# A two-block transformer kernel: the first input loaded a second time in turned layout, scaled, rounded and split by chunk

## The chip, the cores and the metric

One core of one Trainium2 chip. The metric is the device time of one launch in microseconds (us), as the median of several runs. The program names its engines as the profile does: PE (TensorE, the matrix engine), ACT (ScalarE), DVE (VectorE), POOL (GpSimd) and SP (SyncE, which here only issues DMAs).

## The reference

The program computes two transformer blocks, one after the other, on 256 tokens of width 1024, in float32. Only the start of the first block matters here:

```python
def rms_norm(x, g):
    y = x * lax.rsqrt(jnp.mean(x * x, axis=-1, keepdims=True) + EPS)
    return y * g

xn = rms_norm(x, ln_mix_g)           # x: 256 x 1024
proj = xn @ w_in                     # w_in: 1024 x 2560, five blocks of 512 columns
u, v, q, k, vv = five blocks of proj # columns 0.., 512.., 1024.., 1536.., 2048..
a_out = gelu(u) * spatial(rms_norm(gelu(v)))
b_out = banded attention(q, k, vv)
x = x + concat(a_out, b_out) @ w_out
x = x + peer_ffn(rms_norm(x))        # each token gathers 128 rows of a table of experts
```

A second block follows (`second_block`: a pooling branch, a stick-breaking attention, a cross attention, gates and a feed-forward layer). It is untouched by the change.

## The kernel before

**Tiles.** The 256 tokens are two tiles `t` of 128 (`tok(t)`), the width of 1024 is eight chunks `c` of 128. The product of tokens with `w_in` has the chunk's 128 channels on the partitions, so `x` is wanted turned: `aT_hi` and `aT_lo` are 128 partitions x 8 chunks x 256 tokens. The division by the root mean square of a token is put off: it is a factor of a row of the product and is applied after it (`row_scale`, line 857 on). Only the gain `ln_mix_g`, one number per channel (`mix_col`, on the partitions), is multiplied in ahead of the product.

**Three products for one.** To keep float32 accuracy, each operand is split into a rounded part (type fp32r, "hi", ACT) and the rest ("lo", DVE), and `product` (lines 1970 to 1972) issues three matmuls: hi x hi, hi x lo, lo x hi. So every weight block goes through DMA into `wraw` (four slots of 1 MB), a cast on ACT into `w_hi` (line 806), a subtraction on DVE into `w_lo` (line 1288), then PE. A block is half of the 1024 rows of one 512-column part: `in1a` holds chunks 0 to 3, `in1b` chunks 4 to 7 of the first part. Order of the blocks: in1a, in1b, in2a, in2b, in3a, in3b, in4a, in4b, in0a, in0b. Each is 24 matmuls of 512 columns (4 chunks x 2 token tiles x 3). The split has three slots (`S_SLOTS`), and a slot of `wraw` is loaded again when the DVE subtraction of the block in it is done (`load_block`). The blocks in `PIECED` (line 66) are loaded, cast and subtracted in four quarters of 256 KB, one chunk each (lines 618, 813, 1296), and PE waits for each quarter; the others go whole.

**The order of the work** is written out by hand, one list of instructions for each engine, with semaphores between them. At the start:

- SP issues one small load (`const`: the identity, and the columns of the two gains), x tile 0, two quarters of in1a, x tile 1, two more, the four of in1b, then in2a, in2b whole, the rest of the constants, and in3a.
- PE multiplies the identity with itself six times (`keep_warm`, line 1948; 12 records), turns x tile 0 through the identity (`turn_x`, eight transposes at line 1941, into two banks of PSUM), begins in1a, and after its first chunk turns x tile 1 (`between_at=1`).
- DVE multiplies each turned half tile of 128 x 512 by the gain, out of PSUM into `xg` (`gained_T`, line 1326), ACT rounds it into `aT_hi` (`round_x`, line 848), DVE subtracts into `aT_lo` (`rest_x`, line 1333). These steps stand among the quarters of in1a.
- When the splits of in1b and in2a are through, ACT squares and sums x tile 0 and tile 1 from `x_sb` (line 764), takes the roots (line 771), loads the table of the gelu (line 790), casts in2b, takes the gelu of the first product (line 871), squares it, loads the table of the root, and casts in3a and in3b.

After this come attention, the output product, the router, and then `for n in range(ROWS)` 256 gathers of 128 table rows of 8 KB on POOL's queue, each with one dot product on DVE, small steps on ACT and matmuls on PE (line 2284), and after them the second block.

## Time and profile before

| | us |
|---|---|
| median of three runs | 1153.95 |
| lowest, highest | 1153.13, 1154.22 |
| span of the profiled execution, first to last instruction | 1151.8 |

The page gives the profiled execution by its span alone; no device time of its own stands beside it. Shares of the span: PE busy 91%, DVE 67%, ACT 49%, POOL 25%. The chain of waits that ended last runs through PE for 57% of the span and through the DMAs of the gathers for 28%.

How to read it: a timeline row is start, duration, engine, line, operation, operands, count; in brackets the idle time of the engine just before, and what ended it. Durations include what the engine overlaps with the next instruction, so the distance between two starts is often smaller than a duration. PEclk is the clock granted to PE as a share of full speed (1.00 is 2.4 GHz, 0.50 is 1.2 GHz).

### The profile page before, as it was taken

The page shows a single profiled execution, that of the slowest core. Times are in us where ns is not written, and L with a number is a line of the kernel's source. Part 1 is how long each engine was busy: PE and PEld are TensorE (multiplying, and loading weights), DVE is VectorE, ACT ScalarE, POOL GpSimd, SP SyncE. Part 2 cuts the span into 40 slices and gives each one's busy share as a digit, 9 for nine tenths or more (in the row PEclk, how much of TensorE's full clock was granted, in tenths as well). Part 3 has the DMA queues.
Part 4 walks back from the last instruction along what each step waited for, and adds up shares of the span by engine and source line. Part 5 has one row for each costly group of instructions (what it writes and reads, how often), then busy time and mean ns, then how long its engine had stood idle before and what let it go on. Part 6 is the DMA issues. An engine that isn't in the chain of part 4 may idle for free.

```text
span 1151.8 us, 12055 instructions
## 1 busy us (share of the span) xinstructions
PE 1048.5 (91%) x4100; PEld 669.5 (58%) x4100; DVE 770.0 (67%) x1502; ACT 567.0 (49%) x1235; POOL 290.9 (25%) x261
## 2 busy tenths in 40 slices
PE   8999998998899779799887877889999999999998
PEld 7888554454354234344332322349878778888886
DVE  5788777667666657676676665564675496777743
ACT  7664544544543444543444345354765555444432
POOL 0001545544544334454443444400000000000000
PEclk9999999999999999999999999999999999999999
DMA  9848999999999999999999999977433454555540
GB/s 346 346 161 306 420 422 422 421 421 422 421 420 422 420 422 421 411 421 423 422 419 422 423 420 422 422 307 270 181 147 135 157 189 159 183 188 193 195 156 36
DMA packets 55532, 371.87 MB, mean 323 GB/s; under 512 B 6192, under 2 KB 7344, under 8 KB 12080
## 3 DMA queue, kind: packets, MB, share of 16 engines
q0 software_dynamic: 36864, 268.45, 56.1%
q1 hardware_dynamic: 18608, 102.65, 24.1%
q8 instruction: 33, 0.54, 0.2%
q14 instruction: 27, 0.22, 0.1%
HBM read 370.03 MB, written 1.05 MB: 322 GB/s over the span
## 4 chain that ended last, share of the span: by engine, by line
PE 57%; DMA 28%; DVE 6%; ACT 5%; issue 2%; POOL 1%; DVEq 0%; POOLq 0%; ACTq 0%
DMA uv<-in_peer_uv,eidx 28%; PE bank L2284 15%; PE bank L1970 8%; PE bank L1972 8%; PE bank L1971 8%; PE bank L2460 6%; PE bank L2042 4%; PE bank L2459 3%; DVE uv L1579 2%; DVE w_lo L1288 1%; PE bank L1941 1%; ACT diag L1026 1%; POOL uv L730 1%; ACT chosen L1023 1%; PE bank L2160 1%
## 5 line engine op out<-in xcount | busy, mean ns | idle before, releaser
L2284 PE MATMUL bank<-uv,diag 128*128 128x512 f32 x1024 | 486.9, 610 | 89.6 <-ACT diag L1026 89.3
L1579 DVE SCALAR_TENSOR_TENSOR uv<-uv,xn 128x1024 f32<-128x1024 f32 x256 | 313.8, 1226 | 211.7 <-DMA uv<-in_peer_uv,eidx 211.6
L730 POOL DMA_INDIRECT uv<-in_peer_uv,eidx x256 | 290.6, 1135 | 456.3 <-PE bank L2284 329.2
L2284 PEld LDWEIGHTS bank<-uv,diag 128*128 128x128 f32 x1024 | 183.9, 192 | 355.5 <-issue 353.4
L1288 DVE TENSOR_TENSOR w_lo<-wraw,w_hi 128x2048 fp32r<-128x2048 f32 x69 | 157.7, 2290 | 92.2 <-ACT w_hi L806 92.1
L1018 ACT ACTIVATE chosen<-chosen 128x1 f32<-128x1 f32 x256 | 51.8, 202 | 331.7 <-DVE uv L1579 331.3
L806 ACT CAST w_hi<-wraw 128x2048 fp32r<-128x2048 f32 x69 | 131.6, 1908 | 123.6 <-PE bank L2460 62.0
L2460 PE MATMUL bank<-nT_both,w_hi 128*128 128x512 f32 x320 | 109.6, 396 | 0.0
L1026 ACT ACTIVATE diag<-const,chosen 128x128 f32<-128x128 f32 x256 | 102.8, 401 | 8.3
L1023 ACT ACTIVATE chosen<-chosen 128x1 f32<-128x1 f32 x256 | 75.3, 294 | 9.3
L2459 PE MATMUL bank<-nT_both,w_lo 128*128 128x256 f32 x280 | 78.1, 279 | 0.0
L2460 PEld LDWEIGHTS bank<-nT_both,w_hi 128*128 128x128 f32 x320 | 57.3, 188 | 10.8
L1970 PE MATMUL bank<-w_hi,nT_both 128*128 128x512 f32 x144 | 58.0, 403 | 0.9 <-ACT gates L1166 0.6
L1972 PE MATMUL bank<-w_hi,nT_both 128*128 128x512 f32 x144 | 56.2, 390 | 0.0
L1971 PE MATMUL bank<-w_lo,nT_both 128*128 128x512 f32 x144 | 56.2, 390 | 0.0
L2459 PEld LDWEIGHTS bank<-nT_both,w_lo 128*128 128x128 f32 x280 | 52.8, 188 | 1.8
L1970 PE MATMUL bank<-w_hi,aT_hi 128*128 128x512 f32 x104 | 42.1, 404 | 1.8 <-DVE aT_lo L1333 1.8
L1972 PE MATMUL bank<-w_hi,aT_lo 128*128 128x512 f32 x104 | 40.8, 393 | 0.0
L1971 PE MATMUL bank<-w_lo,aT_hi 128*128 128x512 f32 x104 | 40.8, 392 | 0.0
L2042 PEld LDWEIGHTS bank<-bT,wraw 128*128 128x128 f32 x192 | 30.4, 191 | 11.5 <-issue 9.6
L2042 PE MATMUL bank<-bT,wraw 128*128 128x128 f32 (+1 forms) x192 | 34.8, 327 | 0.0
L1970 PE MATMUL bank<-w_hi,hT_hi 128*128 128x512 f32 x88 | 34.2, 389 | 0.0
(331 smaller groups left out, 1371.0 us busy)
## 6 DMA issues: line engine op xcount, KB each, us to landing
wraw<-in_ff_in SPq DMA_DIRECT2D x22, 1024.0 KB, 4.7
wraw<-in_ff_out SPq DMA_DIRECT2D x11, 1024.0 KB, 4.7
wraw<-in_query SPq DMA_DIRECT2D x4, 1024.0 KB, 5.1
uv<-in_peer_uv,eidx POOLq DMA_INDIRECT x256, 15.0
wraw<-in_in_q SPq DMA_DIRECT2D x2, 1024.0 KB, 7.8
wraw<-in_in_k SPq DMA_DIRECT2D x2, 1024.0 KB, 8.3
wraw<-in_pool_o SPq DMA_DIRECT2D x2, 1024.0 KB, 4.6
wraw<-in_sb_o SPq DMA_DIRECT2D x2, 1024.0 KB, 4.7
```

Source lines behind the costliest of these rows:

```text
L730: pool.indirect_dma_start(out=uv[:, RING_AT[n % RING], :], out_offset=None, in_=io["peer_uv"], in_offset=bass.IndirectOffsetOnAxis(ap=eidx ...
L806: nc.scalar.copy(hi, raw).then_inc(w_rounded, 1)
L1026: nc.scalar.activation(diag[:, n % RING, :], ident, ACT.Copy, scale=weight[:, k:k + 1]).then_inc(diag_ready, 1)
L1288: nc.vector.tensor_tensor(lo, raw, hi.bitcast(F32), ALU.subtract).then_inc(w_split, 1)
L1579: nc.vector.scalar_tensor_tensor(out=u, in0=u, scalar=1.0, in1=xn[:, head // PEER_HEADS, :], op0=ALU.mult, op1=ALU.mult, accum_out=hdot[he ...
L1970: nc.tensor.matmul(dst, a_hi, b_hi, start=start, stop=False)
L1971: nc.tensor.matmul(dst, a_hi, b_lo, start=False, stop=False)
L1972: return nc.tensor.matmul(dst, a_lo, b_hi, start=False, stop=stop)
L2042: mm = nc.tensor.matmul(dst[:, a * width:(a + 1) * width], w[:, c * S + a * P:c * S + (a + 1) * P], aT[:, i % 2 * (KC // 2) + c, first:fir ...
L2284: mm = nc.tensor.matmul(acc[m][:, :], diag[:, n % RING, :], uv[:, RING_AT[n % RING], D + m * HALF:D + (m + 1) * HALF], start=False, stop=( ...
L2459: nc.tensor.matmul(*low, start=False, stop=False, skip_group_check=True)
L2460: mm = nc.tensor.matmul(two(dst[:, :]), w_hi[:, w], nT_both[:, :, c, :], start=(c == 0), stop=(c == KC - 1), skip_group_check=True)
```

## The change

`x` comes in a second layout, `xT` (128 partitions x 2 tiles x 8 chunks x 128 tokens), made by the host as it lays out the inputs. It is loaded in four pieces of 256 KB (half a tile's chunks each) straight into `xg`. PE no longer turns x; `keep_warm` runs seven times in place of six and writes bank 0 without asking. ACT rounds by chunk (128 x 128, with the gain as scale) and DVE takes the rest by chunk (one instruction that multiplies by the gain and subtracts), 16 instructions each in place of ACT's four and DVE's four and four. PE waits for each chunk of the first token tile in in1a. `x` by tokens, which ACT's squares and the later sums read, is loaded after in2a. in2a joins `PIECED`.

```diff
--- before.py
+++ after.py
@@ -63,7 +63,7 @@
 SPLIT_AT = {name: n for n, name in enumerate(SPLIT)}
 
 
-PIECED = ("in1a", "in1b", "in2_vb")
+PIECED = ("in1a", "in1b", "in2a", "in2_vb")
 SLOT_AT = {name: (n + (2 if name in ("out1a", "out1b") else n > SPLIT_AT["out1b"])) % S_SLOTS for name, n in SPLIT_AT.items()}
 SLOT_OF = {name: SPLIT[n - S_SLOTS] for name, n in SPLIT_AT.items() if n >= S_SLOTS}
 SLOT_OF |= {f"ff_in{j}": "out2_1b" for j in (2, 3, 4)}
@@ -140,7 +140,8 @@
 
 def psum_uses():
 
-    uses, count, turn, held = {}, [0] * 8, {}, set()
+    uses, count, held = {}, [0] * 8, set()
+    turn = {tuple(range(8)): NT * 2}
 
     def use(*key, among=tuple(range(8))):
         free = [b for b in among if b not in held]
@@ -158,7 +159,6 @@
             for h in range(2):
                 use(name, t, h)
 
-    both("xT")
     for n in (1, 2, 3, 4):
         for t in range(NT):
             use("proj", n, t)
@@ -274,8 +274,7 @@
 
 def rounded_order():
 
-    keys = [("xT", t, h) for h in range(2) for t in range(NT)]
-    keys += [("oT", 0), ("aT", 0), ("aT", 1), ("oT", 1)]
+    keys = [("oT", 0), ("aT", 0), ("aT", 1), ("oT", 1)]
     keys += [("nT", t, h) for t in range(NT) for h in range(2)]
     for i in range(len(SLOT_BLOCKS)):
         if pair_at(i, ATT_SLOT) is not None:
@@ -485,6 +484,8 @@
         rms_ready = sem("rms_ready")
         norm_ready = sem("norm_ready")
         half_normed = sem("half_normed")
+        xT_loaded = [[sem(f"xT_loaded{t}{h}") for h in range(2)] for t in range(NT)]
+        x_rounded = [sem(f"x_rounded{t}") for t in range(NT)]
         x_turned = [sem(f"x_turned{t}") for t in range(NT)]
         w_masked = sem("w_masked")
         bias_masked = sem("bias_masked")
@@ -649,16 +650,24 @@
             def load_x(t):
                 sp.dma_start(x_sb[:, t, :], io["x"][tok(t), :]).then_inc(x_loaded[t], 16)
 
+            def load_xT(t, h):
+                sp.dma_start(xg[:, t, 4 * h:4 * h + 4, :], io["xT"][:, t, 4 * h:4 * h + 4, :]).then_inc(xT_loaded[t][h], 16)
+
             sp.dma_start(const[:, 0:C0], io["const"][:, 0:C0]).then_inc(ident_loaded, 16)
-            load_x(0)
-            for q in range(2):
+            load_xT(0, 0)
+            for q in range(KC // 2):
                 load_piece("in1a", q)
-            load_x(1)
-            for q in range(2, KC // 2):
-                load_piece("in1a", q)
+            load_xT(1, 0)
+            load_piece("in1b", 0)
+            load_xT(0, 1)
+            for q in range(1, KC // 2):
+                load_piece("in1b", q)
+            load_xT(1, 1)
             for q in range(KC // 2):
-                load_piece("in1b", q)
-            load_blocks("in2a", "in2b")
+                load_piece("in2a", q)
+            for t in range(NT):
+                load_x(t)
+            load_block("in2b")
             sp.dma_start(const[:, C0:C0 + 3 * P + 768], io["const"][:, C0:C0 + 3 * P + 768]).then_inc(const_loaded, 16)
             sp.dma_start(cols[:, :], io["cols"]).then_inc(cols_loaded, 16)
             g = io["gmlp_norm_g"]
@@ -840,22 +849,28 @@
 
             act.wait_ge(eps_set, 1)
             load_table(ACT.Sqrt)
-            def round_x(t, h):
-
-                assert rounded["xT", t, h] == turned[0]
-                turned[0] += 1
-                wait_read(act, "xT", t, h)
-                nc.scalar.copy(aT_hi[:, 4 * h:4 * h + 4, tok(t)], xg[:, t, 4 * h:4 * h + 4, :]).then_inc(act_rounded, 1)
-
-            split_piece("in1a", 0)
-            round_x(0, 0)
+            def round_x(t, c):
+
+                if c % 4 == 0:
+                    act.wait_ge(xT_loaded[t][c // 4], 16)
+                nc.scalar.activation(aT_hi[:, c, tok(t)], xg[:, t, c, :], ACT.Copy,
+                                     scale=mix_col[:, c:c + 1]).then_inc(x_rounded[t], 1)
+
+            act.wait_ge(ident_loaded, 16)
+            for q in range(KC // 2):
+                round_x(0, q)
+                split_piece("in1a", q)
+            for c in range(KC // 2):
+                round_x(1, c)
+            split_piece("in1b", 0)
+            for c in range(KC // 2, KC):
+                round_x(0, c)
             for q in range(1, KC // 2):
-                split_piece("in1a", q)
-            for t, h in ((1, 0), (0, 1), (1, 1)):
-                round_x(t, h)
+                split_piece("in1b", q)
+            for c in range(KC // 2, KC):
+                round_x(1, c)
             for q in range(KC // 2):
-                split_piece("in1b", q)
-            split_to("in2a")
+                split_piece("in2a", q)
 
             for t in range(NT):
                 act.wait_ge(x_loaded[t], 16)
@@ -1320,34 +1335,28 @@
 
             nc.vector.memset(small[:, 227:228], 0.0).then_inc(row_free, RING)
 
-            def gained_T(t, h):
-
-                src = wait_full(dve, "xT", t, h)
-                nc.vector.tensor_tensor(xg[:, t, 4 * h:4 * h + 4, :], four(src[:, :]), columns(mix_col, h),
-                                        ALU.mult).then_inc(read_of("xT", t, h), 1)
-
-            def rest_x(t, h):
-
-                dve.wait_ge(act_rounded, rounded["xT", t, h] + 1)
-                where = (slice(None), slice(4 * h, 4 * h + 4), tok(t))
-                nc.vector.tensor_tensor(aT_lo[where], xg[:, t, 4 * h:4 * h + 4, :], aT_hi[where].bitcast(F32),
-                                        ALU.subtract).then_inc(x_turned[t], 1)
+            def rest_x(t, c):
+
+                dve.wait_ge(x_rounded[t], c + 1)
+                nc.vector.scalar_tensor_tensor(out=aT_lo[:, c, tok(t)], in0=xg[:, t, c, :], scalar=mix_col[:, c:c + 1],
+                                               in1=aT_hi[:, c, tok(t)].bitcast(F32), op0=ALU.mult,
+                                               op1=ALU.subtract).then_inc(x_turned[t], 1)
 
             dve.wait_ge(ident_loaded, 16)
-            gained_T(0, 0)
-            split_piece("in1a", 0)
-            rest_x(0, 0)
+            for q in range(KC // 2):
+                rest_x(0, q)
+                split_piece("in1a", q)
+            for c in range(KC // 2):
+                rest_x(1, c)
+            split_piece("in1b", 0)
+            for c in range(KC // 2, KC):
+                rest_x(0, c)
             for q in range(1, KC // 2):
-                split_piece("in1a", q)
-            gained_T(1, 0)
-            gained_T(0, 1)
-            rest_x(1, 0)
-            gained_T(1, 1)
-            rest_x(0, 1)
-            rest_x(1, 1)
+                split_piece("in1b", q)
+            for c in range(KC // 2, KC):
+                rest_x(1, c)
             for q in range(KC // 2):
-                split_piece("in1b", q)
-            split_to("in2a")
+                split_piece("in2a", q)
             for t in range(NT):
                 invert(0, t)
 
@@ -1941,11 +1950,10 @@
                     mm = nc.tensor.transpose(dst[:, c * P:(c + 1) * P], src[:, c * P:(c + 1) * P], ident)
                 mm.then_inc(full_of(*key), 1)
 
-            def keep_warm(turns, *key):
-
-                dst = open_bank(*key)
+            def keep_warm(turns):
+
                 for _ in range(turns):
-                    nc.tensor.matmul(dst[:, 0:P], ident, ident, start=True, stop=True)
+                    nc.tensor.matmul(bank[0][:, 0:P], ident, ident, start=True, stop=True)
 
             def tile_T(n, name, src, t):
 
@@ -1988,13 +1996,16 @@
                 opens = part == 0 if opens is None else opens
                 for t in tiles:
                     if turned == "xT":
-                        pe.wait_ge(x_turned[t], part + 1)
+                        if part or t:
+                            pe.wait_ge(x_turned[t], (part + 1) * (KC // 2))
                     elif turned:
                         wait_read(pe, turned, t, part)
                     dst = open_bank(*key(t)) if opens else bank[at(*key(t))[0]]
                     for c in range(KC // 2):
                         if between and c == between_at and t == 0:
                             between()
+                        if name == "in1a" and t == 0:
+                            pe.wait_ge(x_turned[t], c + 1)
                         if name in PIECED and t == 0:
                             pe.wait_ge(w_split, SPLIT_END[name] - KC // 2 + 1 + c)
                         mm = product(dst[:, :], parts(aT, ALL, c + part * (KC // 2), tok(t)), split_part(name, c),
@@ -2050,19 +2061,10 @@
 
 
             pe.wait_ge(ident_loaded, 16)
-            keep_warm(6, "xT", 0, 0)
-
-            def turn_x(t):
-
-                pe.wait_ge(x_loaded[t], 16)
-                for h in range(2):
-                    transposes(x_sb[:, t, half(h)], "xT", t, h)
-
-            turn_x(0)
+            keep_warm(7)
             for n in (1, 2, 3, 4):
                 for p in "ab":
-                    tokens_out(f"in{n}{p}", aT, lambda t, n=n: ("proj", n, t), turned="xT" if n == 1 else None,
-                               between=(lambda: turn_x(1)) if (n, p) == (1, "a") else None, between_at=1)
+                    tokens_out(f"in{n}{p}", aT, lambda t, n=n: ("proj", n, t), turned="xT" if n == 1 else None)
             for t in range(NT):
                 for name, n, src in (("qT", 2, q_sb), ("kT", 3, k_sb)):
                     wait_read(pe, "proj", n, t)
@@ -2539,6 +2541,7 @@
             blocks(w[n * S:(n + 1) * S], [name], D)
 
     io["x"] = a["x"][0]
+    io["xT"] = a["x"][0].reshape(NT, P, KC, P).transpose(3, 0, 2, 1)
     for n in range(5):
         halves(a["w_in"][:, n * HALF:(n + 1) * HALF], f"in{n}")
     for n in range(2):
```

## Rows read from the trace of the kernel before

**Rows 1.** The page: span, PE's busy time, the chain by engine.
```profile
span 1151.8 us, 12055 instructions
...
PE 1048.5 (91%) x4100; PEld 669.5 (58%) x4100; DVE 770.0 (67%) x1502; ACT 567.0 (49%) x1235; POOL 290.9 (25%) x261
...
PE 57%; DMA 28%; DVE 6%; ACT 5%; issue 2%; POOL 1%; DVEq 0%; POOLq 0%; ACTq 0%
```

**Rows 2.** Busy time by stretch: stretch, length, then each engine's busy time, PEclk, DMA share, GB/s.
```profile
9.30:11.00 1.70, 1.70 (x10) 1.70 (x9) 0.82 (x2) 1.24 (x2) 0.00 (x0) 0.50 0.91 282
...
20.00:30.00 10.00, 10.00 (x46) 8.28 (x45) 3.49 (x4) 9.82 (x16) 0.00 (x0) 1.00 1.03 395
```

**Rows 3.** Timeline of PE, 2 to 34 us.
```profile
2.65 2.93 PE L1948 MATMUL bank<-const 128*128 128x128 f32 x12 [2.65 <-DMA const<-in_const]
...
5.37 1.27 PE L1941 MATMUL bank<-const,x_sb 128*128 128x128 f32 x8
...
8.44 0.50 PE L1970 MATMUL bank<-w_hi,aT_hi 128*128 128x512 f32 x1 [1.80 <-DVE aT_lo L1333]
...
9.24 1.88 PE L1941 MATMUL bank<-const,x_sb 128*128 128x128 f32 x8
...
13.11 0.39 PE L1970 MATMUL bank<-w_hi,aT_hi 128*128 128x512 f32 x1
...
32.97 0.50 PE L1970 MATMUL bank<-w_hi,aT_hi 128*128 128x512 f32 x1
```

**Rows 4.** Timeline of ACT, 6 to 40 us and one row at 126 us.
```profile
6.26 0.62 ACT L813 CAST w_hi<-wraw 128x512 fp32r<-128x512 f32 x1 [4.03 <-DMA wraw<-in_in1a]
...
14.64 2.18 ACT L813 CAST w_hi<-wraw 128x512 fp32r<-128x512 f32 x4
...
18.54 1.05 ACT L764 ACTIVATE junk<-x_sb 128x1024 bf16<-128x1024 f32 x1
...
19.91 1.04 ACT L764 ACTIVATE junk<-x_sb 128x1024 bf16<-128x1024 f32 x1
...
21.39 1.28 ACT L790 ACT_TABLE_LOAD   x1
...
22.80 1.89 ACT L806 CAST w_hi<-wraw 128x2048 fp32r<-128x2048 f32 x1
...
28.70 3.70 ACT L806 CAST w_hi<-wraw 128x2048 fp32r<-128x2048 f32 x2
...
126.31 0.40 ACT L1026 ACTIVATE diag<-const,chosen 128x128 f32<-128x128 f32 x1
```

**Rows 5.** Timeline of DVE, 24 to 36 us and one row at 101 us.
```profile
24.79 2.29 DVE L1288 TENSOR_TENSOR w_lo<-wraw,w_hi 128x2048 fp32r<-128x2048 f32 x1 [3.15 <-ACT w_hi L806]
...
30.62 4.49 DVE L1288 TENSOR_TENSOR w_lo<-wraw,w_hi 128x2048 fp32r<-128x2048 f32 x2 [3.54 <-ACT w_hi L806]
...
101.09 0.29 DVE L1629 TENSOR_TENSOR onehot<-onehot,small 128x128 f32<-128x128 f32 x1
```

**Rows 6.** DMA issues by tensor: engine operation, duration, first and last start; us to landing.
```profile
L650 SPq DMA_DIRECT2D x_sb<-in_x x2: 417/424/432, 1.2 to 2.6; - x2
...
DMA to landing us min/median/max: 3.7/5.0/6.3
...
L618 SPq DMA_DIRECT2D wraw<-in_in1a x4: 423/432/505, 1.7 to 3.5; - x4
...
DMA to landing us min/median/max: 4.6/5.7/6.6
...
L618 SPq DMA_DIRECT2D wraw<-in_in1b x4: 512/578/655, 4.1 to 5.9; - x4
...
DMA to landing us min/median/max: 6.9/7.2/7.3
...
L631 SPq DMA_DIRECT2D wraw<-in_in2b x1: 432/432/432, 7.2 to 7.2; - x1
...
DMA to landing us min/median/max: 11.0/11.0/11.0
```

## The prediction

> **What bounds the kernel now.** I read the page first: PE is busy for 91% of the span, and the chain that ended last runs through PE for 57% and the gathers' DMAs for 28% [rows 1]. The first gather needs the router, which needs everything before it, so a microsecond won on the chain from the start to the router should move the whole program by one, if nothing behind it soaks it up. The change touches only the first 35 us. Next came busy time by stretch: from 20 to 30 us PE is busy for all 10.00 us, and ACT for 9.82 [rows 2]. PE works without a gap, yet ACT has no room either. That is what the reader has to see: two engines are full, and a gain on one is worth what the other lets through. The timelines show how near they are. In the steady stream a block of 24 matmuls lasts 5.44 us (in1a to in2b are 96 matmuls; the tenth starts at 13.11 and in3a's first at 32.97, so 87 starts take 19.86 us, of which 0.1 is a wait: 0.227 each) [rows 3]. Counted back from the tenth matmul at 13.11, the stream behaves as if it had begun at 13.11 - 9 x 0.227 = 11.07 us. So PE wants in2b at 11.07 + 3 x 5.44 = 27.4 and in3a at 32.8. DVE finishes in2b's rest at 24.79 + 2.29 = 27.08 and in3a's at 30.62 + 2.29 = 32.91 [rows 5]. **PE has 0.3 us to spare at in2b and none at in3a.** DVE is idle 3.15 and 3.54 us before these, waiting for ACT's casts at 22.80 and 28.70 [rows 4, 5]. ACT's casts of in2b and in3a are thus a second chain as tight as PE's.
>
> **What it removes from PE.** Before the first product: keep_warm to 5.58, transposes to 6.64, then a wait of 1.80 for gain, rounding and rest, to 8.44; after three matmuls eight more transposes of 1.88; PE's clock stands at 0.50 from 9.30 to 11.00, that is 1.2 GHz, after that wait [rows 2, 3]. All this goes.
>
> **When data land.** The loads form one queue, so I count bytes ahead and use landings as the curve. x tile 0 lands at 1.2 + 3.7 = 4.9 with 584 KB (72 + 512) ahead and in it, x tile 1 at 2.6 + 6.3 = 8.9 (1608 KB), in1a's last quarter at 3.5 + 6.6 = 10.1 (2120), in1b's last at 5.9 + 7.3 = 13.2 (3144), in2b at 7.2 + 11.0 = 18.2 (5192) [rows 6]. The rate is 256 KB/us from 584 to 1608, 330 in the quarters of in1b, 410 in whole blocks.
> In the new order xT's first piece is at 328 KB (about 4.0 us), in1a's first quarter at 584 (4.9), its last at 1352 (8.0), the second xT piece 1608 (8.9), in1b's first 1864 (9.5), its last 2888 (12.5), the last xT piece 3144 (13.2). in2a's quarters come at 330 KB/us rather than 410: 13.2 + 1024/330 = 16.3 for the last. x tile 1 comes at 5192 KB, the place of in2b before: 18.2 + 0.6 for the quarters = 18.8. in2b, one MB later, at 21.3; in3a at 25.8. SP issues seven DMAs more ahead of in2b, at some 0.5 us each (durations 0.42 to 0.65), so in2b goes out near 11 instead of 7.2; it lands ten later, so SP's queue is not the bound [rows 6].
>
> **ACT.** A quarter's cast takes 0.52 from start to start ((2.18 - 0.62)/3) [rows 4]. A 128x128 ACTIVATE with a scale column takes 0.40, about 0.30 to the next [rows 4]: 16 x 0.30 = 4.8 us replace four roundings of 0.52 = 2.1, and in2a costs 2.1 rather than about 1.8. That is 3.0 us more work, but ACT starts sooner (x at 4.0 instead of a quarter at 6.26). Walking the list: in1a's quarters cast at 4.95, 6.1, 7.1, 8.0 with a chunk of x between each; x tile 1 from 8.95; in1b's first at 10.2; the last xT chunk ends 14.8; in2a's last cast ends 16.9. Then ACT must wait for x tile 0 (17.5) and tile 1 (18.8), which before lay in SBUF since 8.9. From the square of tile 1 to the cast of in2b it is 22.80 - 19.91 = 2.89 us [rows 4]. Square at 18.9, cast at **21.8 instead of 22.80: one microsecond gained**. in2b is there (21.3). In3a's cast follows 5.90 later [rows 4]: 27.7, and its data land at 25.8. DVE's rest ends one us earlier too: 26.1 for in2b, 31.9 for in3a.
> The small ACTIVATE has no exact row: below, it is nearly free, which gains nothing as DMA ends last; above, it costs what a 128x512 does, 0.52, 3.5 us more in all, of which 0.6 is covered by the wait for x tile 0, and some 2 to 3 come through. I take 0.30, the row of its shape.
>
> **DVE.** 128x128 takes 0.29 and 128x2048 takes 2.29 [rows 5], on that line 128x512 takes 0.69, 0.09 less from start to start. Sixteen rests at 0.20 are 3.2 us where eight instructions of 0.6 were (4.8). Hidden: DVE waits for ACT throughout.
>
> **PE after.** keep_warm is one matmul longer, 2.93/6 = 0.49, to 6.1. First quarter: cast at 4.95 ends 5.6, rest ends 6.3, PE starts at 6.35 instead of 8.44. Chunks then come at 7.5, 8.5, 9.4 (as DVE finishes quarters); tile 1's four chunks of x are rested at 10.6; in1a ends 13.4, in1b 18.8, in2a 24.3. PE's stream is 3.1 us ahead (7.9 against 11.07). Then it waits: in2b is ready at 26.1. **A wait of 1.9 us for ACT's cast takes the place of the one removed.** in2b ends 31.6, in3a starts at 32.0 instead of 32.97. Sum: 1.0 us faster. The edits of bank turns, semaphores and the uncounted wait on bank 0 I put at nothing; keep_warm's cover is the load of in1a, and without it would cost its 0.49. All loads up to the end of this burst land one MB, 2.5 us, later. Each later block is wanted 5.44 us after the last and loads in 2.5, so this is made good within one block; behind in3a I price it at nothing, at most 1.
>
> **A rule against it.** The quarters of in1b landed 0.6 to 0.9 us apart, though each took about 7 us from issue, as they overlap [rows 6]. The Trainium skill (DMA: Bandwidth & Descriptors, Bandwidth) says transfers should be batched to at least 1 MiB; its fit elsewhere on the page gives every DMA a fixed 2 us. Were these 2 us paid one after the other by in2a's three extra quarters, x tile 1 would come 6 us later and the program would be 5 slower, by an estimate from that page. The rows speak against paying it in series: it has 0.02 of the second rival's chance, whose own mechanism is a low rate, not a fixed cost.
>
> **Rivals.**
> *One: PE's lead is kept whole.* If loads run faster than I say (x tile 1 by 16.7 us), or ACT's wait proves shorter, in3a starts at 7.9 + 21.8 = 29.8: 3.1 us gained, 1150.8. For: PE does lose 3.1 us now. Against: DVE's idle 3.15 and 3.54 before the two blocks. A part way, all quarters at 340 KB/us from the start, gives 2.3.
> *Two: x by tokens comes too late, and it is slower.* Place: ACT's square of x tile 1, before in2b's cast. It decides from a landing of 19.8 us (then in2b's cast is where it was). If every 256 KB transfer goes at 250 KB/us, the slow stretch of the curve, the 4096 KB of quarters take 16.4 us from 2.9, x tile 1 comes at 21.8 and in2b is cast 2.0 later than now: 1155.9; with a dearer small ACTIVATE on top, up to 1157. For: all loads ahead are 256 KB pieces now, and that slow stretch held them. Against: 330 in the later quarters.
> *Three: the clock falls at the new wait.* After the wait of 1.80 PE ran at 1.2 GHz; the new one, 1.9 us, is as long. In the old case the half clock reached from 9.30 to past 11.00 [rows 2]. If it takes three or four us of in2b, these matmuls take double: 1.7 us lost, in3a starts at 33.3, 0.3 later than before: 1154.2.
> *Four: the gain is taken off later*, by the gathers or the loads that are 2.5 us late: 1154.0, within one either way.
>
> **How the numbers follow.** The profile's span is 1151.8, and the median is 2.15 above it; I take 1.0 off both: span 1150.8, median 1152.9. A measurement of this kernel can tell about 0.2%, 2.3 us. Chances: forecast 0.43; rival one 0.15, faster by over 0.2%; two 0.22, of which 0.11 is over 2.3 us and the rest within; three 0.14, same; four 0.06, of which 0.02 falls on each side. Faster 0.17, same 0.70, slower 0.13. The range takes in rival one at its full gain and two at its price of 2.0: 1150.6 to 1155.9.
>
> **What would show it.** Right: no transposes of x; first product near 6.4; casts of in1a follow one another by about 1.0; PE idle 1 to 2 us before in2b with DVE's w_lo as releaser; in2b's cast near 21.8, in3a's near 27.7, PE at 1.00 in the first 24 us. Wrong: no wait at in2b (rival one); a square of x tile 1 after 19.9 (two); 0.50 granted behind the wait (three); in3a's start 1 us earlier but the first gather not (four).

## The result, and the profile after

The changed kernel takes 1156.36 us (median of 8 runs, 1154.93 to 1158.89) against 1153.97 (8 runs, 1153.13 to 1154.68): a ratio of 1.0023, 95% interval 1.0014 to 1.0032. It is slower by 2.4 us where 1.0 us less was forecast, and outside the range. The profiled execution took 1155.86 with a span of 1154.0; the span before was 1151.8 [rows 1], so the two profiles differ by 2.2 and can be read against each other.

The page of the changed kernel: span, busy time, and the chain by engine.

```profile
span 1154.0 us, 12062 instructions
...
PE 1052.6 (91%) x4086; PEld 670.4 (58%) x4086; DVE 770.2 (67%) x1513; ACT 570.1 (49%) x1250; POOL 291.1 (25%) x261
...
PE 55%; DMA 30%; DVE 6%; ACT 5%; issue 2%; SPq 1%; POOL 0%; DVEq 0%; POOLq 0%; ACTq 0%
```

The page does not say where the time went: the shares of [rows 1] have moved by 2 points at most. SPq is new among them. The timeline of PE in the changed kernel answers to [rows 3].

```profile
2.60 3.36 PE L1956 MATMUL bank<-const 128*128 128x128 f32 x14 [2.60 <-DMA const<-in_const]
7.21 0.76 PE L1978 MATMUL bank<-w_hi,aT_hi 128*128 128x512 f32 x1 [1.26 <-DVE w_lo L1311]
7.78 0.63 PE L1979 MATMUL bank<-w_lo,aT_hi 128*128 128x512 f32 x1
8.20 0.63 PE L1980 MATMUL bank<-w_hi,aT_lo 128*128 128x512 f32 x1
...
10.26 0.40 PE L1979 MATMUL bank<-w_lo,aT_hi 128*128 128x512 f32 x1
...
27.29 0.79 PE L1978 MATMUL bank<-w_hi,aT_hi 128*128 128x512 f32 x1 [2.10 <-DVE w_lo L1303]
...
34.44 0.39 PE L1978 MATMUL bank<-w_hi,aT_hi 128*128 128x512 f32 x1
...
56.20 0.60 PE L1950 MATMUL bank<-const,q_sb 128*128 128x128 f32 x4
```

The transposes are gone and the first product starts 1.23 us earlier than 8.44. Its first seven matmuls stand some 0.43 apart, the later ones 0.23. The eighth starts at 10.26, so the steady stream behaves as if it had begun at 10.26 - 7 x 0.227 = 8.67 instead of 11.07: a lead of 2.4 us. It runs without a gap to in2b, and there PE waits 2.10 us for VectorE. in3a's first matmul is at 34.44 instead of 32.97, and the q and k transposes, at 54.86 before, are at 56.20. The lead of 2.4 has become a loss of 1.5 at in3a and 1.3 at the transposes. Busy time by stretch shows the rest of it (columns as in [rows 2]):

```profile
7.21:10.26 3.05, 3.04 (x7) 2.43 (x8) 2.68 (x7) 2.60 (x8) 0.00 (x0) 1.00 1.03 307
20.00:30.00 10.00, 7.90 (x29) 6.10 (x29) 2.62 (x3) 9.82 (x16) 0.00 (x0) 0.86 1.04 400
25.19:27.29 2.10, 0.00 (x1) 0.00 (x1) 2.05 (x1) 2.01 (x6) 0.00 (x0) 0.98 0.99 406
27.29:30.60 3.31, 3.31 (x8) 2.63 (x9) 0.00 (x0) 3.28 (x5) 0.00 (x0) 0.50 1.06 358
30.60:34.00 3.40, 3.40 (x17) 2.77 (x16) 3.23 (x2) 2.52 (x3) 0.00 (x0) 1.00 1.03 403
```

PE now has 7.90 of 10 us, where [rows 2] had 10.00, and ACT the same 9.82. Behind the wait PE's granted clock is 0.50, so 1.2 GHz, for 3.31 us: 8 matmuls in it where 3.31/0.227 = 14.6 would fit, 1.5 us lost. The timelines of ACT and then of VectorE answer to [rows 4, 5]:

```profile
3.98 0.40 ACT L856 ACTIVATE aT_hi<-xn,const 128x128 fp32r<-128x128 f32 x1 [1.75 <-DMA xn<-in_xT]
5.73 0.62 ACT L822 CAST w_hi<-wraw 128x512 fp32r<-128x512 f32 x1 [1.34 <-DMA wraw<-in_in1a]
...
18.69 1.06 ACT L773 ACTIVATE junk<-x_sb 128x1024 bf16<-128x1024 f32 x1 [0.61 <-DMA x_sb<-in_x]
...
20.07 1.04 ACT L773 ACTIVATE junk<-x_sb 128x1024 bf16<-128x1024 f32 x1
...
22.95 1.89 ACT L815 CAST w_hi<-wraw 128x2048 fp32r<-128x2048 f32 x1
...
28.85 3.69 ACT L815 CAST w_hi<-wraw 128x2048 fp32r<-128x2048 f32 x2
...
41.41 1.91 ACT L815 CAST w_hi<-wraw 128x2048 fp32r<-128x2048 f32 x1 [4.29 <-DMA wraw<-in_in4b]
```

```profile
24.94 2.29 DVE L1303 TENSOR_TENSOR w_lo<-wraw,w_hi 128x2048 fp32r<-128x2048 f32 x1 [3.15 <-ACT w_hi L815]
30.77 4.50 DVE L1303 TENSOR_TENSOR w_lo<-wraw,w_hi 128x2048 fp32r<-128x2048 f32 x2 [3.53 <-ACT w_hi L815]
```

Every row of these two engines from 18 to 31 us is where it was before, within 0.16: squares at 18.54 and 19.91, casts at 22.80 and 28.70, rests at 24.79 and 30.62 [rows 4, 5]. **This chain has not gained anything.** And one row behind it is new: the cast of in4b came at 38.79 before, when PE had freed a slot of the split for it; now it is at 41.41, after 4.29 us of waiting for its data. Before:

```profile
38.79 1.91 ACT L806 CAST w_hi<-wraw 128x2048 fp32r<-128x2048 f32 x1 [3.28 <-PE bank L1972]
```

SyncE's issues read, in the kernel before:

```profile
20.99 2.10 SPq L631 DMA_DIRECT2D wraw<-in_in4a  x1
...
27.11 0.33 SPq L631 DMA_DIRECT2D wraw<-in_in4b  x1
```

and of the changed one:

```profile
11.38 0.44 SPq L632 DMA_DIRECT2D wraw<-in_in2b  x1
...
19.07 8.33 SPq L632 DMA_DIRECT2D wraw<-in_in4a  x1
...
28.40 0.43 SPq L632 DMA_DIRECT2D wraw<-in_in4b  x1
```

in4a's issue holds SyncE for 8.33 us instead of 2.10, and in4b goes out 1.29 later, with 13.0 us from there to its landing where it was 11.0: it lands at 41.4 instead of 38.1. The long issue is the smaller part of this. in4b's slot comes free at 24.94 + 2.29 = 27.23, and SyncE is held until 27.40; then the second bias and a gain go out ahead of it. What counts is the queue, which is full all the time. Busy time by stretch from 12 us until in4b is nearly in, before and after:

```profile
12.00:38.70 26.70, 26.70 (x116) 21.75 (x116) 18.40 (x19) 22.35 (x30) 0.00 (x0) 0.99 1.03 412
```

```profile
12.00:41.30 29.30, 27.20 (x114) 22.03 (x113) 17.03 (x23) 22.17 (x34) 0.00 (x0) 0.94 1.04 409
```

The loads issued up to and with in4b are 12688 KB before and 13712 now. The added MB takes 1.05 MB / 0.41 MB/us = 2.6 us at these rates, and 3.3 were measured; the DMA share of 1.03 and 1.04 says that no pause was there to take it up. The shift at the start then goes through to the gathers: the first one is at 102.27 before (first row) and 103.59 after (second).

```profile
102.27 1.09 POOL L730 DMA_INDIRECT uv<-in_peer_uv,eidx  x1 [101.29 <-DVE eidx L1570]
```

```profile
103.59 1.08 POOL L739 DMA_INDIRECT uv<-in_peer_uv,eidx  x1 [102.61 <-DVE eidx L1579]
```

That is 1.3 of the 2.2 us. From the first gather's issue to the last it was 644.60 us and is 645.43, 0.8 more, and from there to the end 404.9 and 405.0.

### The profile page after: what moved, and what is told of

It is laid out like the page before. It is cut to its first block, busy times and chain, and to the rows that moved or that the text cites. A ratio compares the mean times of both kernels' runs of the same rounds, so it can differ in the third digit from the quotient of the medians.

```text
span 1154.0 us, 12062 instructions
## 1 busy us (share of the span) xinstructions
PE 1052.6 (91%) x4086; PEld 670.4 (58%) x4086; DVE 770.2 (67%) x1513; ACT 570.1 (49%) x1250; POOL 291.1 (25%) x261
## 3 DMA queue, kind: packets, MB, share of 16 engines
HBM read 371.08 MB, written 1.05 MB: 322 GB/s over the span
## 4 chain that ended last, share of the span: by engine, by line
PE 55%; DMA 30%; DVE 6%; ACT 5%; issue 2%; SPq 1%; POOL 0%; DVEq 0%; POOLq 0%; ACTq 0%
DMA uv<-in_peer_uv,eidx 29%; PE bank L2286 15%; PE bank L1978 7%; PE bank L1980 7%; PE bank L1979 7%; PE bank L2462 6%; PE bank L2053 4%; PE bank L2461 3%; DVE uv L1588 2%; DVE w_lo L1303 1%; DMA wraw<-in_in2b 1%; PE bank L1950 1%; ACT diag L1041 1%; ACT chosen L1038 1%; ACT w_hi L815 1%
```

## The experiments

Of every kernel the text gives the median, the ratio to the kernel before measured beside it, with its 95% interval, and the start of the first gather ("gather at"), where all that happens in the first 100 us comes together. The ratio rests on 8 to 12 executions, the gather on the profile of one, and the two do not always agree: two kernels below with the same loads and the same median (1154.14 and 1154.18) have it at 103.60 and 102.20, and the kernel before has it at 102.27 in one profile and 102.59 in another. A difference in it of up to 1.4 us proves nothing by itself. The three theories at first: the wait at in2b and the half clock behind it cost the time; the quarters of in2a do; the order of x by tokens and in2a in the queues does.

**Keep PE busy during the wait.** Nine matmuls into bank 0 ahead of in2b, nothing else:

```diff
                 for p in "ab":
+                    if (n, p) == (2, "b"):
+                        keep_warm(9)
                     tokens_out(f"in{n}{p}", ...)
```

> The changed kernel, with nine matmuls of the identity with itself (2.1 us at 0.118 us a record, 18 records) put on TensorE where it waits for in2b. Theory A (the clock, which stood at 0.50 behind the wait of 2.10 us, is what turns a standstill into a loss): in2b still starts near 27.3 us, runs at 1.00 throughout, ends near 32.8, in3a starts near 33.1 instead of 34.3, and the program takes 1.2 to 1.5 us less than the changed kernel, near 1155.0, 0.1% above the kernel before. Theory B (the loss is made behind in3a, by the late loads or in the gathers): no change against the changed kernel, 1156.4, whatever the clock does.

1155.75 us, ratio 1.0018 (1.0009 to 1.0026), gather at 104.14. The clock stayed at 1.00 and the q and k transposes came 1.0 us earlier than in the changed kernel, but the gather did not, and the time was 1.0018 against 1.0023, which the intervals do not tell apart. PE and then ACT, of this kernel:

```profile
55.20 0.60 PE L1950 MATMUL bank<-const,q_sb 128*128 128x128 f32 x4
...
69.77 1.27 PE L1950 MATMUL bank<-const,prob 128*128 128x128 f32 x8 [1.33 <-DVE prob L1435]
```

```profile
42.46 1.91 ACT L815 CAST w_hi<-wraw 128x2048 fp32r<-128x2048 f32 x1 [4.35 <-DMA wraw<-in_in4b]
```

PE was ahead until the attention, and there it waited 1.33 us for VectorE's prob, whose list ran late since in4b came late. So the loss has two limits of almost the same size, and taking away one shows the other.

**x by tokens ahead of in2a's quarters**, in the loads and in the lists of ACT and VectorE:

```diff
-            for q in range(KC // 2):
-                load_piece("in2a", q)
             for t in range(NT):
                 load_x(t)
+            for q in range(KC // 2):
+                load_piece("in2a", q)
```

> The changed kernel, with x by tokens loaded ahead of in2a's quarters rather than behind them, and its squares, roots and the gelu's table done on ScalarE (and the inverse on VectorE) ahead of in2a's splits. If in2b's cast waits for ScalarE's squares, the cast moves from 22.95 to in2b's landing (22.4), no more, since the bytes ahead of in2b are the same; in2a comes 2.5 us later, so TensorE's wait splits in two shorter ones, at in2a and in2b. Theory A: neither is long enough to lower the clock, and the program takes 1 to 2 us less than the changed kernel, 1154.5 to 1155.4. Theory B: it stays at 1156.4.

1156.13, 1.0020 (1.0011 to 1.0029), gather at 103.69. **in2a in one piece**, the rest as in the changed kernel:

```diff
-PIECED = ("in1a", "in1b", "in2a", "in2_vb")
+PIECED = ("in1a", "in1b", "in2_vb")
```

> The changed kernel, with in2a loaded and split whole, as before. If the quarters cost landing time, x by tokens and in2b land up to 0.6 us earlier (x tile 1 from 19.3 to 18.7, in2b from 22.4 to 21.8), but in2a is ready later, so ScalarE comes to the squares no earlier. Theory A and B both: within 0.5 us of the changed kernel; a gain of over 1 us would say that the quarters were the fault.

1156.14, 1.0016 (1.0007 to 1.0025), gather at 103.15. Both moved the wait to in2a. PE's timeline in the first and in the second, and the stretch from 24 to 27 us of each:

```profile
21.91 0.50 PE L1977 MATMUL bank<-w_hi,aT_hi 128*128 128x512 f32 x1 [2.20 <-DVE w_lo L1310]
```

```profile
21.41 0.50 PE L1975 MATMUL bank<-w_hi,aT_hi 128*128 128x512 f32 x1 [1.98 <-DVE w_lo L1301]
```

```profile
24.00:27.00 3.00, 3.00 (x9) 2.38 (x8) 2.29 (x1) 2.91 (x6) 0.00 (x0) 0.56 1.03 427
```

```profile
24.00:27.00 3.00, 3.00 (x14) 2.27 (x13) 1.82 (x1) 2.91 (x6) 0.00 (x0) 1.00 1.00 410
```

After the wait of 2.20 us the clock fell (0.56 granted from 24 to 27 us, 1.00 still from 21.9 to 22.9), after that of 1.98 it did not, and the time was the same. The order of x and in2a makes no difference that the intervals show.

**in2b loaded, cast and subtracted ahead of x by tokens**; ACT also casts in3a ahead of the squares of vg:

```diff
-            for t in range(NT):
-                load_x(t)
             load_block("in2b")
+            for t in range(NT):
+                load_x(t)
```

> The changed kernel, with in2b loaded ahead of x by tokens, cast on ScalarE ahead of the squares (rest on VectorE ahead of the inverses), and in3a cast after the gelu and ahead of the squares of its result. In2b should land near 20, be ready near 24.3, and TensorE should not wait for it at all; in3a lands near 26, is cast near 27.1 and is ready near 31.4, 1.1 us after in2b's end. Theory A: no wait over 1.3 us, no half clock after the start, in3a starts 1.0 to 1.6 us earlier than in the kernel before, and the program is 1.0 to 1.5 us faster than that, 1152.4 to 1153.0. Theory B: in3a starts earlier, and the program is not faster than 1154.

1157.17, 1.0028 (1.0018 to 1.0039), gather at 103.55. PE and ACT of this kernel:

```profile
31.94 0.50 PE L1978 MATMUL bank<-w_hi,aT_hi 128*128 128x512 f32 x1 [1.07 <-DVE w_lo L1302]
...
69.20 1.27 PE L1950 MATMUL bank<-const,prob 128*128 128x128 f32 x8 [1.74 <-DVE prob L1435]
```

```profile
41.88 1.91 ACT L815 CAST w_hi<-wraw 128x2048 fp32r<-128x2048 f32 x1 [4.35 <-DMA wraw<-in_in4b]
```

No wait at in2b and in3a 1.0 us earlier than before, just the gain that was forecast; and it is lost again at prob, behind the late cast of in4b. This kernel's twelve times spread from 1155.04 to 1160.33, so that its median is rough.

**The late in4b mended as well.** The kernel just told, with the loads that nothing needs soon put behind in4b:

```diff
-            sp.dma_start(bias0[:, :, :], io["rel"][:, :, P:S]).then_inc(a_loaded, 16)
-            load_block("in4a")
-            sp.dma_start(bias1[:, :, :], io["rel"]).then_inc(a_loaded, 16)
-            load_gain(1, "norm_mem_2")
-            load_blocks("in4b", "in0b")
+            load_blocks("in4a", "in4b")
+            sp.dma_start(bias0[:, :, :], io["rel"][:, :, P:S]).then_inc(a_loaded, 16)
+            sp.dma_start(bias1[:, :, :], io["rel"]).then_inc(a_loaded, 16)
+            load_gain(1, "norm_mem_2")
+            load_blocks("in0a", "in0b")
```

> The kernel with in2b ahead of x by tokens, and besides this in4a and in4b loaded ahead of the two bias tables and the gain, that is 2 MB of loads that are wanted late go behind them. Theory C (the late in4b is the second limit: it landed at 41.9 us, ScalarE stood 4.35 us for it, and VectorE's list up to the attention came 1.5 us behind TensorE, which then waited 1.74 for the probabilities): in4b lands before 38, ScalarE does not wait for it, TensorE does not wait before turning the probabilities, the spatial product starts near 68.2 us instead of 70.30 (69.00 in the kernel before), and the first gather near 101.4 instead of 103.55. Theory D (something else holds the attention back): the first gather stays near 103.5. Time by C: 1153.2 if the gathers take as long as in the kernel before, 1154.2 if they keep the 0.8 to 1.0 us that every variant added there.

1153.97, 0.9999 (0.9990 to 1.0008), gather at 101.49, 2.1 us earlier than in the kernel without this edit, whose ratio was 1.0028. SyncE and ACT of this kernel:

```profile
19.18 0.33 SPq L632 DMA_DIRECT2D wraw<-in_in4a  x1
24.26 0.33 SPq L632 DMA_DIRECT2D wraw<-in_in4b  x1
24.63 1.44 SPq L679 DMA_DIRECT2D bias<-in_rel  x1
26.11 6.10 SPq L680 DMA_DIRECT2D bias<-in_rel  x1
```

```profile
38.02 1.91 ACT L815 CAST w_hi<-wraw 128x2048 fp32r<-128x2048 f32 x1 [0.58 <-PE bank L1980]
```

The long issue is still there, 6.10 us, but behind in4b, where nothing waits for it. in4b's cast waits for PE again, and PE no longer waits for prob. With the **same edit on the kernel with the nine matmuls** (in2b behind x):

> The changed kernel with the nine matmuls in the wait for in2b, and in4a and in4b ahead of the bias tables and the gain. Theory C: the second limit is gone, so that keeping the clock up shows in the time: in3a starts near 33.1 us, the first gather near 102.4 instead of 104.14, and the program takes 1.5 to 1.8 us less than with the nine matmuls alone, near 1154.1, the time of the kernel before plus what the gathers add. Theory D: near 1155.7 as with the nine matmuls alone.

1154.80, 1.0006 (0.9997 to 1.0015), gather at 102.62; without this edit it was 1.0018 and 104.14. And **on the kernel before alone**:

> The kernel before with in4a and in4b loaded ahead of the bias tables and the gain, and nothing else. In it in4b is cast when TensorE frees its slot (38.79), not when it lands (38.1), so that loading it earlier should do nothing: 1154.0 within 0.4. Then e11's gain belongs to the turned x with the new order. A gain of over 1 us would say that the order alone gives it.

1153.81, 0.9998 (0.9989 to 1.0007), gather at 102.31: there in4b is not late, and the edit gives nothing.

**What does one MB more cost by itself?** The kernel before, with the new input put second in the list of inputs, as in the changed kernel, and loaded into a buffer that nothing reads, between in2a and in2b:

```diff
-            load_blocks("in2a", "in2b")
+            load_block("in2a")
+            sp.dma_start(spare[:, :], io["xT"]).then_inc(spare_loaded, 16)
+            load_block("in2b")
```

> The kernel before, and one more load: x turned, 1 MB, into a tile that nothing reads, between in2a and in2b. Theory C (bytes and the order of loads): in2b lands near 20.8, still ahead of its cast at 22.8, in4b near 41, past ScalarE's 38.8 but with VectorE still waiting for the second product; the start of the gathers moves by 0 to 0.5 us. If the extra 0.8 to 1.0 us of the gathers belong to the longer queue or the one more input, they show here (gathers 645.4 from first to last issue instead of 644.6) and the time is 1154.8 to 1155.5; if they belong to the rest of the change, the time is within 0.5 of the kernel before.

1156.09, 1.0016 (1.0007 to 1.0025), gather at 103.73: nearly the whole loss of the changed kernel, with nothing else of the change. ACT's timeline of this kernel has in2b cast 1.5 us later than before, and in4b cast after a wait for its data, 1.9 later:

```profile
24.26 1.89 ACT L811 CAST w_hi<-wraw 128x2048 fp32r<-128x2048 f32 x1
...
40.70 1.91 ACT L811 CAST w_hi<-wraw 128x2048 fp32r<-128x2048 f32 x1 [3.79 <-DMA wraw<-in_in4b]
```

Here in4a's issue took 3.90 us, and in4b went out at 28.57, as soon as its slot was free; it still landed at 40.7. The bytes ahead of it are enough to make it late.

But the loads ahead of the added one came later too: in1a's last quarter took 8.0 us from issue instead of 6.6 [rows 6]. The kernel before once more, measured beside it,

> The kernel before, unchanged, for the spread of a profile: whether the time from the first to the last issue of the gathers, 644.60 us in its one profile, repeats within 0.3 us, or varies by as much as the 0.8 to 1.1 by which the changed kernels exceed it. Time 1154.0 within 0.5.

gave 1154.00 (0.9999, 0.9990 to 1.0008), gather at 102.59. That pointed to something that holds from the first microsecond: the new input is the second in the list of inputs. If the inputs lie in memory in the order of the list, every one behind it lies one MB further on; the order is what the runs below change, and the addresses themselves were not looked at. **Only in2a's quarters, in the kernel before,** cost little:

```diff
-PIECED = ("in1a", "in1b", "in2_vb")
+PIECED = ("in1a", "in1b", "in2a", "in2_vb")
```

> The kernel before, with in2a in quarters and nothing else. The quarters add 0.6 us to in2b's landing (18.2 to 18.8), still 4 us ahead of its cast; ScalarE spends 2.1 us on in2a rather than 1.8. Its cast of in2b, and with it in3a, come 0.2 to 0.5 us later, and TensorE's start of in3a with them: 0.2 to 0.5 us slower than the kernel before. Over 1 us would say that the quarters carry the loss.

1154.70, 1.0004 (0.9995 to 1.0013), gather at 103.74. The profiled execution was the slowest of the eleven (1155.61), with in2b cast at 24.21; by its start alone the quarters would cost as much as the whole change, by the median they do not.

**The changed kernel with xT as its last input**, so that all others keep their place in the list; the program itself is not edited:

```diff
     io["x"] = a["x"][0]
-    io["xT"] = a["x"][0].reshape(NT, P, KC, P).transpose(3, 0, 2, 1)
...
+    io["xT"] = a["x"][0].reshape(NT, P, KC, P).transpose(3, 0, 2, 1)
     return {k: np.ascontiguousarray(v) for k, v in io.items()}
```

> The changed kernel, with the turned copy of x as the last of the inputs rather than the second, so that every other input keeps its place in memory; the program is the same. The gathers took 644.60 and 644.80 us from first to last issue in the two profiles of the kernel before, and 645.28 to 646.05 in the seven kernels with the extra input. Theory E (place in memory): they return to 644.6 to 644.9, and the time falls by 0.7 to 1.0 to 1155.5. Theory F (not the place): 645.3 or more, and 1156.4.

1154.52, 1.0007 (0.9998 to 1.0016), gather at 103.42: 1.8 us less than the changed kernel. In its profile the wait at in2b is 1.00 and the clock stays at 1.00, but in4b is cast at 41.75, still after 4.36 us of waiting for data. **The kernel before with xT as second input**, loaded only late (ahead of `query7`), and read by nothing:

```diff
+            sp.dma_start(spare[:, :], io["xT"]).then_inc(spare_loaded, 16)
+            sp.wait_ge(spare_loaded, 16)
             load_apart("query7")
```

> The kernel before, with the turned copy of x as its second input and loaded once (1 MB) into a tile that nothing reads, but only behind the weights of the attention and the router, when the DMA engines are idle. The start is then that of the kernel before. Theory E (place in memory): first gather near 102.4 us, gathers 645.3 or more, time 1154.7 to 1155.0. Theory F: gathers 644.6 to 644.9, time 1154.0. If the first microseconds are slower as well (with the extra load early, in1a's last quarter landed 8.0 us after its issue, not 6.6), the place of the inputs matters for the early loads too.

1155.72, 1.0015 (1.0006 to 1.0024), gather at 102.77: 1.5 us more. Two more have the same late load, with its input elsewhere in the list; nothing reads it there either. **Last of all inputs:**

> The kernel before, with the extra input last and read late: nothing moves in memory, the late load alone is added. If the place is the cause of e10's 1.5 us, this one takes 1154.0 to 1154.4. If it takes 1155.5, the late load is the cause and the place is not.

1154.18, 1.0002 (0.9993 to 1.0011), gather at 102.20. So the late load is free. **Right ahead of the table peer_uv**, so that the table has one more MB ahead of it and the weights do not:

> The kernel before, with the extra input of 1 MB placed right ahead of the experts' table and read late, so that of the larger inputs only the table moves in memory and the weights stay. Theory G (the table's place costs): gathers 645.3 or more, 1155.0 to 1155.7, like e10. Theory H (the weights' place costs, or only the early loads): gathers 644.5 to 644.9 and 1154.1.

1154.14, 1.0000 (0.9991 to 1.0009), gather at 103.60. So the table's place is not it either: the cost comes when the inputs between x, which is first and never moves, and the table are shifted, the weights among them.

**The parts together.** The kernel with in2b ahead, in4b mended and **xT as last input**:

> The kernel with in2b ahead of x by tokens and the bias tables behind in4b, with the turned x as the last input. Theory E: first gather near 101.5 us as before, gathers 644.7, time 1153.2, 0.9 us faster than the kernel before. Theory F: 1154.0.

1152.64, 0.9989 (0.9980 to 0.9998), gather at 101.33: the fastest, 1.5 us under the kernel before, and 1.3 under the same program with xT second. And the changed kernel as it is, with only **in4b mended and xT last**:

> The change as it was made, with the turned x as the last input and in4a and in4b ahead of the bias tables. Theory C: with the second limit gone, the wait at in2b is all that is left. If it stays near 1.0 us and the clock at full speed as in e9, in3a starts 0.5 us ahead of the kernel before, the first gather comes near 101.8, and the time is 1153.5; if it is 2 us and the clock falls, the first gather comes near 103.5 and the time is 1155. Without theory C it stays at e9's 1154.5.

1153.29, 0.9996 (0.9987 to 1.0005). PE, ACT and POOL of this kernel:

```profile
26.41 0.50 PE L1978 MATMUL bank<-w_hi,aT_hi 128*128 128x512 f32 x1 [1.02 <-DVE w_lo L1303]
...
67.22 1.20 PE L1950 MATMUL bank<-const,prob 128*128 128x128 f32 x8
```

```profile
22.08 1.89 ACT L815 CAST w_hi<-wraw 128x2048 fp32r<-128x2048 f32 x1
...
38.37 1.91 ACT L815 CAST w_hi<-wraw 128x2048 fp32r<-128x2048 f32 x1 [2.60 <-PE bank L1980]
```

```profile
101.53 1.09 POOL L739 DMA_INDIRECT uv<-in_peer_uv,eidx  x1 [100.55 <-DVE eidx L1579]
```

With both repaired the forecast's picture is there: in2b's cast 0.7 us earlier than before, a wait of 1.0 and no half clock behind it, the first gather 0.74 earlier. Its time is too near the kernel before to be told from it by the interval.

## Why the prediction was wrong

**Held.** PE needs no transposes; the new wait is at in2b, released by VectorE's w_lo, and 2.10 us long where 1.9 was forecast; a small rounding takes 0.40 and 0.30 to the next; SyncE's queue is not what holds in2b, which goes out at 11.4 (11 forecast). A shift at the start passes to the gathers, with nothing soaking it up. The rule that small transfers cost much did not decide: in2a's quarters alone gave 1.0004 (0.9995 to 1.0013), and undoing them in the changed kernel 1156.14 against 1156.36. The Trainium skill (DMA: Bandwidth & Descriptors, Bandwidth) wants at least 1 MiB in a transfer for 75% of the peak rate; four of 256 KB in a full queue show no cost near the 5 us that the prediction worked out as an estimate.

**Sizes in the first 25 us.** The first product came at 7.21, not 6.35: ACT's cast of in1a's first quarter was at 5.73, waiting for data that I had at 4.9. The rest on VectorE takes 0.34, not 0.29, which is hidden. PE's lead was 2.4 of the 3.1 forecast, and the missing 0.7 is this late start. I counted the half clock of [rows 2] as something that goes, and something of its size came back in another place: the first seven matmuls are 0.43 apart, 10.26 - 7.21 - 7 x 0.227 = 1.5 us, about as much as the 7.9 - 6.35 that I had put down for chunks that come one by one. The half clock was no fixed cost of the kernel before, either: its second profile has 1.00 granted from 8.00 to 12.60, and its q and k transposes are at 55.20, later than the 54.86 of the first.

**The step "Cast at 21.8 instead of 22.80: one microsecond gained" failed.** It was at 22.95. Its inputs were landings from a curve: x tile 1 at 18.8, in2b at 21.3. Measured were a first square at 18.69, bound by x tile 0 (17.5 forecast), and in2b at 11.4 + 11.0 = 22.4. Both are 1.1 to 1.2 late, which is the whole gain. Part of this goes with the place of the new input: in2b is cast at 22.95, 22.95 and 22.99 in the three profiles with this order of loads and xT second, and at 22.24 and 22.08 in the two with xT last.

**Three rivals share what happened.** Rival three was right in its mechanism: the wait was followed by 1.2 GHz for 3.31 us, 1.5 us of loss against the 1.7 that it named. It had 0.14, though the only wait of such a length in the trace of before had shown just this [rows 3]. By itself it would not have decided either, as the nine matmuls show. Rival two's sign came too: the square of x tile 1 at 20.07, past 19.9, after a landing at 10.9 + 9.1 = 20.0, with its threshold at 19.8; but only at the threshold, so that in2b's cast is where it was and not 2.0 later. Rival four, with 0.06, named the loads that are late by one MB, and its sign (in3a 1 us earlier and the first gather not) is what the kernel with in2b ahead shows: 31.94 and 103.55. The range ended at 1155.9, since it took in no two of them together.

**The step "behind in3a I price it at nothing, at most 1" failed.** in4b lands 3.3 us later (41.4 against 38.1), and its cast moves from 38.79, where PE released it, to 41.41. It had 0.7 us to spare before, the MB costs 2.6. I had argued that one block is wanted per 5.44 us and loads in 2.5, so that the delay is made good within one block. But the queue has more in it than blocks (constants, two biases and a gain, 3.3 MB from in2b to in4b), and it moved 412 GB/s without a pause before the change: there was nothing in it that could make the delay good. Taking 2 MB of these from ahead of in4b brought its landing from 41.7 to 36.5 in the kernel with xT last (28.74 + 13.0 and 26.39 + 10.1), 5.2 us, which is about 2 MB at this rate. In three pairs of kernels this edit gave 1.0028 to 0.9999, 1.0018 to 1.0006 and 1.0007 to 0.9996, and in the kernel before, where in4b is not late, nothing.

**Nothing in the prediction allowed for the place of the inputs.** It is as large as any part shown: changed kernel to the same with xT last, 1.0023 to 1.0007; with in2b ahead and in4b mended, 0.9999 to 0.9989; kernel before with the late load, 1.0015 with its input second and 1.0002 with it last. These are 1.2 to 1.8 us, of a loss of 2.4; each pair of intervals overlaps a little, and all three pairs go the same way. A single profile does not say where the time goes, but all eighteen together say something. From the first gather's issue to the last it was 644.87 to 646.05 us, 645.5 on average, in the nine with the input second, and 644.25 to 645.31, 644.7 on average, in the nine without it or with it elsewhere. So 0.8 us of it comes behind the start, where the prediction had no term at all. Which of the moved inputs it is, and by what mechanism, stays open.

**Accounting,** by the ratios, one edit at a time from the changed kernel: with xT last, 1.0023 becomes 1.0007, so the place is 1.8 us. With in4b mended as well, 1.0007 becomes 0.9996 (the gather 103.42 becomes 101.53), so the late in4b is 1.2 to 1.3. What is left is 0.5 under the kernel before, half of the 1.0 forecast, and no change by its interval. Each ratio is known to 0.0009, 1 us, so the two prices are rough. The half clock has no step of its own: in the profile with xT last the wait was 1.00 and no half clock followed, so what of its 1.5 us came through would lie in the step of the place. A gain at PE alone (the nine matmuls, or in2b ahead) gave nothing while in4b was late. The changed kernel with in4b mended and xT second was not run; the nearest to it, with the nine matmuls besides, has 1.0006.

## What to carry to other kernels

When an edit adds a load at the start, count for every later load the bytes ahead of it in the queue, and hold its new landing against the instruction that waits for it. A queue that never pauses passes the delay on to the first load with less room than that, here in4b with 0.7 us. When two engines are within 0.3 us of each other, undoing the loss on one shows only the other, so test the pair. A new input goes last in the list of inputs, or its place is tested by itself, before a difference of 0.1 to 0.2% is put down to the program. And a difference of about 1 us in a single profile is held against the medians before it is believed.

## What had not been expected of the hardware

- The place of an added input in the list of inputs changes this kernel's time by 0.1 to 0.16%: 1.0015 (1.0006 to 1.0024) for an input of 1 MB put second and used late, 1.0002 (0.9993 to 1.0011) for the same put last.
- An issue on SyncE is not always 0.3 to 0.6 us: in4a's took 8.33 behind the first load of the bias, 3.90 in the kernel before with one MB more, and 0.33 where the bias stood behind it; then the bias's second load took 6.10. What sets it is not shown.
- A wait of 2.10 or 2.20 us on PE was followed by 1.2 GHz, one of 1.98 was not, and one of 1.80 before the change was [rows 2, 3], and so was one of 1.86 at the second chunk of the fastest kernel (0.50 granted from 10 to 12 us). Length alone does not tell, in these runs.
- At the first product PE's matmuls stood 0.43 apart, the spacing of the stretch at 0.50 behind in2b's wait, though the profile's granted clock there is 1.00 (7.21 to 10.26). The kernel with the input ahead of the table has the same from 12.31 to 14.87, and its first gather at 103.60. Their spacing is the safer reading.
